# Memory key/value weights through two pairs of raw buffers, and the first two memory query tiles in another product order

## The chip, the cores and the metric

The kernel runs on one core of one Trainium2 chip. The metric is the device time of one execution in microseconds (us). Three executions of the kernel before took 1806.55, 1808.07 and 1809.97 us; the median is 1808.07.

## The reference, cut to what matters

One step of a decoder layer for a prompt of 512 tokens and 8 sample sequences of 8 tokens, so T = 576 token columns in all, D = 1024 features. Three branches (an SSD mixer, block-sparse attention, attention into a memory of 256 tokens) are fed from one input projection, gated, projected and added; a feed-forward block with a short convolution follows. The change lies where the memory branch begins:

```
mkv = (_rmsnorm(mem_prompt, mem_norm_w[l]) @ w_mem_kv[l]).reshape(b_p, n_mem, 2, MEM_HEADS, MEM_HEAD_DIM)
mk_p, mv_p = mkv[:, :, 0], mkv[:, :, 1]
...
y_mem = _mem_attend(qm, mem_k, mem_v)
```

`mem_prompt` has 256 rows; `w_mem_kv` is 1024 x 2048, which is 16 tiles of 1024 x 128. `qm` is a 1024-column part of the input projection of all 576 columns, 8 tiles.

## The kernel before

All dense weights go through one stream of tiles of 1024 x 128 (512 KB), laid out in the order of use. Tile n belongs to parity n % 2, and each parity has one raw buffer (`w_raw`), one pair of split buffers (`w_hi`, `w_lo`) and one PSUM pair (`dps`). fp32 products are made of three reduced-precision ones, high by high, high weight by low activation, and low weight by high activation, 8 contraction steps each.

A tile passes through four queues. SP loads it (`load`, L2543) once the tile before it of the same parity has been split (`w_split`). GpSimd (POOL) waits until TensorE (PE) has finished that earlier tile (`dense_full`) and the load has landed (`w_landed`), writes `w_hi` (L2556), then the difference `w_lo` in four pieces (L2560). PE multiplies (`pe_dense`, L206) in one of two orders: whole, where it waits for `w_hi` alone, makes all products with `w_hi` first (L217) and waits for `w_lo` only then (L222); or in parts, where it waits for both halves and makes the three products step by step (L237).

In the memory stage the 16 key/value tiles (`n_mem` on, called m = 0 to 15 here) are 256 columns wide, so a tile costs PE 24 matmuls where the tiles around it cost 48. There POOL writes only `w_hi` (`split_high`, L2563), and VectorE (DVE) writes `w_lo` (`dve_mem_weight`, L1953), which is what signals `w_split`. Two of these DVE steps stand in the stage before, the block attention's end (`gate1_done` counts its eight merged tiles, L1873): the one of m = 0 behind merged tile 6, that of m = 1 behind merged tile 7. ScalarE (ACT) copies each result out of PSUM (L1984) and issues four loads of `vc` among them (L1988).

Then follow the eight query tiles (`n_qm`, q0 to q7 here), two for each of four heads. `pe_h` (L2104) makes q0 and q1 in parts, with 16 transposes of the memory values between them (`pe_mem_turns`, L1964), before the first head's scores.

Of the kernel before, what the change touches and what calls it, by code (L numbers as in the profile page):

```python
# [16 lines left out]
F32 = mybir.dt.float32  # L17
F32R = mybir.dt.float32r
ALU = mybir.AluOpType
# [4 lines left out]
P = 128  # L24
D = 1024
KT = D // P
SEQ = 512
NB, DT = 8, 8
# [95 lines left out]
def build_program(nc, io):  # L124
    ctx = ExitStack()
    with ctx:
# [3 lines left out]
        def stage_sb(stack, name, shape, dt=F32):  # L130
            return stack.enter_context(nc.sbuf_tensor(name, shape, dt))

        def sem(name):
            return ctx.enter_context(nc.semaphore(name))
# [6 lines left out]
        merged = sb("merged", [P, KT, T])  # L141
        w_raw = sb("w_raw", [P, 2, D])
        w_hi, w_lo = sb("w_hi", [P, 2, D], F32R), sb("w_lo", [P, 2, D], F32R)
        w_taken = sem("w_taken")

        era = ExitStack()
        dt_tok = stage_sb(era, "dt_tok", [P, 2, CH + 1, HEADS])
# [20 lines left out]
        psY = ctx.enter_context(nc.psum_tensor("psY", [P, 512], F32))  # L168


        w_landed = [sem("w_landed0"), sem("w_landed1")]
        w_hi_done = sem("w_hi_done")
        w_split = [sem("w_split0"), sem("w_split1")]
        dense_full = [sem("dense_full0"), sem("dense_full1")]
# [1 line left out]
        cst_in, fea_in, x_in = sem("cst_in"), sem("fea_in"), [sem("x_in0"), sem("x_in1")]  # L176
        out_done = sem("out_done")
        dve_step, act_step = sem("dve_step"), sem("act_step")
        stage_done = [sem("pe_stage"), sem("act_stage"), sem("dve_stage")]

        chains = {}

        ended = [0, 0, 0]

        def stage_end(e, own):

            ended[own] += 1
            count = ended[own]
            e.drain().then_inc(stage_done[own], 1)
            for other in range(3):  # L190
                e.wait_ge(stage_done[other], count)

        def from_one(count):

            return count + 1
# [6 lines left out]
        def slot(n0, u, i=0, nb=0):  # L202

            return (n0 + u) % 2, (n0 + u) // 2 + i * (nb // 2)

        def pe_dense(pe, tile, hi, lo, nk=KT, width=T, ready=None, part=None):  # L206


            par, k0 = tile
            if part is None and ready is None:  # L210
                pe.wait_ge(w_hi_done, k0 * 2 + par + 1)
                pe.wait_ge(dense_free[par], k0)
                spans = [(0, 0, width)] if width <= 512 and width != T else [(0, 0, HALF), (1, HALF, HALF)]
                for k in range(nk):
                    for j, a in enumerate((hi, lo)):
                        for b, c0, cw in spans:
                            pe.matmul(dps[:, par, b, 0:cw], w_hi[:, par, k * P:(k + 1) * P], a[:, k, c0:c0 + cw],  # L217
                                      start=(k == 0 and j == 0), stop=False)
                pe.wait_ge(w_split[par], from_one(k0 + 1))
                for k in range(nk):  # L220
                    for b, c0, cw in spans:
                        mm = pe.matmul(dps[:, par, b, 0:cw], w_lo[:, par, k * P:(k + 1) * P], hi[:, k, c0:c0 + cw],  # L222
                                       start=False, stop=(k == nk - 1))
                mm.then_inc(dense_full[par], 1)
                return
            first, end = part or (0, nk)
            if first == 0:
                pe.wait_ge(w_split[par], from_one(k0 + 1))
                pe.wait_ge(dense_free[par], k0)
            spans = [(0, 0, width)] if width <= 512 and width != T else [(0, 0, HALF), (1, HALF, HALF)]  # L230
            for k in range(first, end):
                if ready:
                    pe.wait_ge(*ready[k])
                wh, wl = w_hi[:, par, k * P:(k + 1) * P], w_lo[:, par, k * P:(k + 1) * P]
                for j, (w, a) in enumerate(((wh, hi), (wh, lo), (wl, hi))):
                    for b, c0, cw in spans:
                        mm = pe.matmul(dps[:, par, b, 0:cw], w, a[:, k, c0:c0 + cw],  # L237
                                       start=(k == 0 and j == 0), stop=(k == nk - 1 and j == 2))
            if end == nk:
                mm.then_inc(dense_full[par], 1)  # L240
# [1648 lines left out]
        kc = ms("kc", [P, NB, 2, MEM])  # L1889
        vc = ms("vc", [P, NB, 2, MEM])  # L1890
        mk = ExitStack()
        stage_sb(mk, "apart_m", [P, 2744])
        mem_hi, mem_lo = (stage_sb(mk, f"mem_{k}", [P, KT, MEM], F32R) for k in ("hi", "lo"))
        memx = stage_sb(mk, "memx", [P, KT, MEM])
        mk.close()
# [57 lines left out]
        def dve_mem_weight(dve, n):  # L1953

            dve.wait_ge(w_hi_done, n + 1)
            par = n % 2
            dve.tensor_tensor(w_lo[:, par, :], w_raw[:, par, :], w_hi[:, par, :].bitcast(F32), ALU.subtract).then_inc(w_split[par], 1)

        def pe_mem(pe):
            pe.wait_ge(mem_lo_ready, mem_at["lo"] + KT)  # L1960
# [52 lines left out]
        n_qm = take(KT)  # L2013
# [90 lines left out]
        def pe_h(pe):  # L2104
            def ahead(h, u, part):
                if h < 4:
                    pe_dense(pe, slot(n_qm, 2 * h + u), xn_hi, xn_lo, part=part)

            ahead(0, 0, (0, KT))
            pe_mem_turns(pe)  # L2110
            ahead(0, 1, (0, KT))
            pe.wait_ge(vmt_copied, 4)
            for h in range(4):
                for u in range(2):
                    par, k0 = slot(n_qm, 2 * h + u)
                    pe.wait_ge(dense_free[par], k0 + 1)
                pe_scores_h(pe, h, 0)
                pe_scores_h(pe, h, 1)
                pe_scores_h(pe, h, "sample")
                ahead(h + 1, 0, (0, KT // 2))  # L2120
                pe_turn_h(pe, h, 0)
                pe_scores_h(pe, h, 2)
                pe_turn_h(pe, h, 1)
                pe_scores_h(pe, h, 3)
                ahead(h + 1, 0, (KT // 2, KT))
                pe_turn_h(pe, h, "sample")
                pe_turn_h(pe, h, 2)
                ahead(h + 1, 1, (0, KT // 2))
                pe_values_s(pe, h)
                pe_turn_h(pe, h, 3)  # L2130
                ahead(h + 1, 1, (KT // 2, KT))
                pe_values_h(pe, h)
                pe_out_s(pe, h)
# [406 lines left out]

        block = ctx.enter_context(nc.Block())
        n_tiles = nstream[0]
        def load(sp, i, par):  # L2543

            sp.wait_ge(w_split[par], from_one(i))
            sp.dma_start(w_raw[:, par, :], io["wstream"][bass.ds(i * 2 + par, 1), :, :].rearrange("o p c -> (o p) c")).then_inc(w_landed[par], 16)
# [1 line left out]
        def load_tile(sp, n):  # L2548
            load(sp, n // 2, n % 2)

        def split(pool, i, par):

            pool.wait_ge(dense_full[par], from_one(i))
            pool.wait_ge(w_landed[par], i * 16 + 16)
            pool.sem_inc(w_taken, 1)
            pool.tensor_scalar(w_hi[:, par, :], w_raw[:, par, :], 1.0, 1.0, ALU.mult, ALU.mult).then_inc(w_hi_done, 1)  # L2556
            pool.wait_ge(w_hi_done, i * 2 + (par + 1))
            for piece in range(4):
                at = slice(piece * D // 4, (piece + 1) * D // 4)
                ins = pool.tensor_tensor(w_lo[:, par, at], w_raw[:, par, at], w_hi[:, par, at].bitcast(F32), ALU.subtract)  # L2560
            ins.then_inc(w_split[par], 1)

        def split_high(pool, i, par):  # L2563

            pool.wait_ge(dense_full[par], from_one(i))
            pool.wait_ge(w_landed[par], i * 16 + 16)
            pool.sem_inc(w_taken, 1)
            pool.tensor_scalar(w_hi[:, par, :], w_raw[:, par, :], 1.0, 1.0, ALU.mult, ALU.mult).then_inc(w_hi_done, 1)

        def split_tile(pool, n):  # L2570
            split(pool, n // 2, n % 2)
# [1 line left out]
        def stream(eng, one, first, end):  # L2573

            if first % 2:
                one(eng, first // 2, 1)
            with eng.Fori((first + 1) // 2, end // 2) as i:
                for par in range(2):
                    one(eng, i, par)
            if end % 2:  # L2580
                one(eng, end // 2, 0)

        @block.sync
        def _(sp):
            sp_load(sp)
            stream(sp, load, 0, n_gate1 + 2)
            sp_pages(sp)
            stream(sp, load, n_gate1 + 2 + NB, n_tiles)
            for written, count in final_waits:
                sp.wait_ge(written, count)  # L2590

        @block.gpsimd
        def _(pool):

            pool.sem_inc(w_split[0], 1)
            pool.sem_inc(w_split[1], 1)
            stream(pool, split, 0, 2)
            norm1.pool(pool)
            stream(pool, split, 2, n_gate1 + 2)
            pool_pages(pool)  # L2600
            stream(pool, split, n_gate1 + 1 + NB, n_mem)
            stream(pool, split_high, n_mem, n_mem + 2 * KT)
            stream(pool, split, n_mem + 2 * KT, n_ffn + 3)
            norm2.pool(pool)
            stream(pool, split, n_ffn + 3, n_tiles)

        @block.tensor
        def _(pe):
# [278 lines left out]
```

## Time and profile before

| | |
|---|---|
| median of three runs | 1808.07 us |
| profiled execution, span | 1812.1 us |
| PE busy | 1742.6 us (96%) |
| DVE, ACT, POOL busy | 924.8, 614.5, 972.8 us |
| mean granted TensorE clock | 0.985 of full speed |
| chain that ended last | PE 89%, DVE 4%, DMA 3%, ACT 2% |

The page shows nothing of the profiled execution outside its span, from the first instruction to the last. Matmuls overlap in the array: one of 256 columns is listed with 0.28 us, but the next one starts 0.12 us later, so costs of PE are read from start to start.

### The profile page before, as it was taken

The page shows a single profiled execution, that of the slowest core. Times are in us where ns is not written, and L with a number is a line of the kernel's source. Part 1 is how long each engine was busy: PE and PEld are TensorE (multiplying, and loading weights), DVE is VectorE, ACT ScalarE, POOL GpSimd, SP SyncE. Part 2 cuts the span into 40 slices and gives each one's busy share as a digit, 9 for nine tenths or more (in the row PEclk, how much of TensorE's full clock was granted, in tenths as well). Part 3 has the DMA queues.
Part 4 walks back from the last instruction along what each step waited for, and adds up shares of the span by engine and source line. Part 5 has one row for each costly group of instructions (what it writes and reads, how often), then busy time and mean ns, then how long its engine had stood idle before and what let it go on. Part 6 is the DMA issues. An engine that isn't in the chain of part 4 may idle for free.

```text
span 1812.1 us, 35702 instructions
## 1 busy us (share of the span) xinstructions
PE 1742.6 (96%) x13888; PEld 1608.6 (89%) x13888; DVE 924.8 (51%) x1558; ACT 614.5 (34%) x1652; POOL 972.8 (54%) x1088
## 2 busy tenths in 40 slices
PE   6999999999999999998999989999999999999997
PEld 6889889899998998885777988779999999999997
DVE  6776677722774334665564731221246761562454
ACT  4355545513554201554442112321024430331231
POOL 4544544555454465211453534226676886886765
PEclk9999999999999999998999999999999999999998
DMA  4113231223213233013786265532222222222222
GB/s 162 62 56 109 98 107 59 97 79 112 95 61 108 96 101 108 25 47 127 268 302 226 81 198 192 192 135 82 82 82 70 82 82 82 82 82 82 82 82 108
DMA packets 53605, 198.48 MB, mean 110 GB/s; under 512 B 6353, under 2 KB 7378, under 8 KB 49874
## 3 DMA queue, kind: packets, MB, share of 16 engines
q1 hardware_dynamic: 41618, 133.36, 22.6%
q10 hardware_dynamic: 7200, 47.81, 7.2%
q0 software_dynamic: 4640, 15.21, 2.4%
q8 instruction: 110, 1.80, 0.4%
q14 instruction: 37, 0.30, 0.0%
HBM read 180.43 MB, written 15.92 MB: 108 GB/s over the span
## 4 chain that ended last, share of the span: by engine, by line
PE 89%; DVE 4%; DMA 3%; ACT 2%; issue 1%; POOL 1%; POOLq 0%; DVEq 0%; SPq 0%; ACTq 0%
PE dps L217 36%; PE dps L222 18%; PE dps L237 16%; DMA w_raw<-wstream_dram 1%; DMA pages<-kv_pages_dram 1%; PE psLE L1645 1%; PE psY L538 1%; PE psLE L588 1%; PE psY L555 1%; PE psY L1366 1%; PE psY L1668 1%; PE psLE L2090 1%; PE psLE L2052 1%; PE psA L1356 1%; PE psY L609 1%
## 5 line engine op out<-in xcount | busy, mean ns | idle before, releaser
L2560 POOL TENSOR_TENSOR w_lo<-w_raw,w_hi 128x256 fp32r<-128x256 f32 x804 | 697.6, 897 | 16.8
L2556 POOL TENSOR_SCALAR w_hi<-w_raw 128x1024 fp32r<-128x1024 f32 x201 | 219.1, 1090 | 663.3 <-PE dps L222 382.6
L217 PE MATMUL dps<-xn_hi,w_hi 128*128 128x288 f32 x1504 | 324.6, 298 | 5.0 <-ACT cbuf L714 4.0
L217 PE MATMUL dps<-xn_lo,w_hi 128*128 128x288 f32 x1504 | 326.2, 299 | 0.0
L217 PEld LDWEIGHTS dps<-xn_hi,w_hi 128*128 128x128 f32 x1504 | 248.4, 191 | 7.9 <-issue 5.3
L217 PEld LDWEIGHTS dps<-xn_lo,w_hi 128*128 128x128 f32 x1504 | 242.6, 190 | 0.0
L222 PE MATMUL dps<-xn_hi,w_lo 128*128 128x288 f32 x1504 | 215.6, 296 | 0.0
L222 PEld LDWEIGHTS dps<-xn_hi,w_lo 128*128 128x128 f32 x1504 | 205.7, 189 | 0.0
L217 PE MATMUL dps<-y_lo,w_hi 128*128 128x288 f32 x808 | 175.0, 298 | 0.0
L217 PE MATMUL dps<-y_hi,w_hi 128*128 128x288 f32 x808 | 173.0, 296 | 0.5 <-POOL w_hi L2556 0.5
L237 PE MATMUL dps<-xn_hi,w_hi 128*128 128x288 f32 x656 | 153.4, 316 | 7.3 <-DVE xn_lo L339 4.1
L237 PE MATMUL dps<-xn_hi,w_lo 128*128 128x288 f32 x656 | 143.4, 301 | 0.0
L237 PE MATMUL dps<-xn_lo,w_hi 128*128 128x288 f32 x656 | 142.8, 300 | 0.0
L237 PEld LDWEIGHTS dps<-xn_hi,w_hi 128*128 128x128 f32 x656 | 106.9, 194 | 31.9 <-issue 23.5
L217 PEld LDWEIGHTS dps<-y_hi,w_hi 128*128 128x128 f32 x808 | 132.3, 190 | 0.9 <-POOL w_hi L2556 0.8
L217 PEld LDWEIGHTS dps<-y_lo,w_hi 128*128 128x128 f32 x808 | 129.6, 189 | 0.0
L222 PE MATMUL dps<-y_hi,w_lo 128*128 128x288 f32 x808 | 116.2, 296 | 0.0
L222 PEld LDWEIGHTS dps<-y_hi,w_lo 128*128 128x128 f32 x808 | 110.6, 189 | 0.0
L237 PEld LDWEIGHTS dps<-xn_lo,w_hi 128*128 128x128 f32 x656 | 108.4, 194 | 0.0
L237 PEld LDWEIGHTS dps<-xn_hi,w_lo 128*128 128x128 f32 x656 | 108.0, 193 | 0.0
L875 DVE SCALAR_TENSOR_TENSOR cout<-cbuf,fea,cout 128x600 f32<-128x600 f32 x96 | 81.9, 854 | 43.1 <-ACT cout L718 40.6
L2469 DVE SCALAR_TENSOR_TENSOR fout<-fin,fea,fout 128x592 f32<-128x592 f32 x44 | 46.7, 1062 | 91.7 <-ACT fout L2455 91.7
(402 smaller groups left out, 2778.8 us busy)
## 6 DMA issues: line engine op xcount, KB each, us to landing
w_raw<-wstream_dram SPq DMA_DIRECT2D x217, 512.0 KB, 3.5
pages<-kv_pages_dram SPq DMA_DIRECT2D x70, 256.0 KB, 3.8
pages<-kv_pages_dram POOLq DMA_DIRECT2D x58, 256.0 KB, 4.0
st_in<-state_t_dram ACTq DMA_DIRECT2D x8, 1024.0 KB, 4.8
ssm_s_dram<-st_in ACTq DMA_DIRECT2D x8, 1024.0 KB, 4.2
kc<-mem_kt_dram ACTq DMA_DIRECT2D x4, 2048.0 KB, 8.8
vc<-mem_v_dram ACTq DMA_DIRECT2D x3, 2048.0 KB, 7.9
h_res<-x_t_dram ACTq DMA_DIRECT2D x1, 2304.0 KB, 9.1
```

Of the source, the lines that this page charges most:

```text
L217: pe.matmul(dps[:, par, b, 0:cw], w_hi[:, par, k * P:(k + 1) * P], a[:, k, c0:c0 + cw], start=(k == 0 and j == 0), stop=False)
L222: mm = pe.matmul(dps[:, par, b, 0:cw], w_lo[:, par, k * P:(k + 1) * P], hi[:, k, c0:c0 + cw], start=False, stop=(k == nk - 1))
L237: mm = pe.matmul(dps[:, par, b, 0:cw], w, a[:, k, c0:c0 + cw], start=(k == 0 and j == 0), stop=(k == nk - 1 and j == 2))
L538: pe.matmul(o, xdt[0:m, h * 64:h * 64 + 64], lv[:, h, :], start=True, stop=not carried)
L555: pe.matmul(psY[:, 256:512], btok[:], xdtd[:], start=True, stop=True).then_inc(y_full, 1)
L588: mm = pe.matmul(psLE[:, half, 0:256], bm[rows, half * 4 + r, :], xds[rows, :], start=True, stop=True)
L609: mm = pe.matmul(gsum[:, c:c + 1], xg_of(G)[:, j, at], ones[:, 0:1], start=(j == 0), stop=(j == halves - 1))
L875: ins = dve.scalar_tensor_tensor(co, cb[:, j:j + CW - PAD], w(j), co, ALU.mult, ALU.add)
L1356: mm = pe.transpose(turn_bank(n)[:, k * P:(k + 1) * P], probs(i)[:, hh, kt * P:(kt + 1) * P], ident)
L2469: link(dve.scalar_tensor_tensor(fo, fb[:, 1:1 + FO], tap_of("fconvw", p, u, 1, FCONV), fo, ALU.mult, ALU.add))
L2556: pool.tensor_scalar(w_hi[:, par, :], w_raw[:, par, :], 1.0, 1.0, ALU.mult, ALU.mult).then_inc(w_hi_done, 1)
L2560: ins = pool.tensor_tensor(w_lo[:, par, at], w_raw[:, par, at], w_hi[:, par, at].bitcast(F32), ALU.subtract)
```

## The change

A second raw pair `w_more` is laid into a stretch of on-chip memory that the memory stage had left unused, and which holds buffers of the block attention until that ends. The 16 key/value tiles use `w_raw` for m = 0, 1, 4, 5, 8, 9, 12, 13 and `w_more` for the others. A load waits for the split of the tile four before it rather than two; the load of m = 2 waits also for `gate1_done` to reach eight, since it is the first to write `w_more`. The first two loads behind the stage, q0 and q1, wait in the same way for m = 12 and 13. The sixteen loads and high splits are written out rather than looped. q0 and q1 are called without `part`, so that they use the whole order. An unused function and its semaphores go.

```diff
+        w_more = stage_sb(mk, "w_more", [P, 2, D])
-        stage_sb(mk, "apart_m", [P, 2744])
+        stage_sb(mk, "apart_m", [P, 2744 - 2 * D])
...
-            dve.tensor_tensor(w_lo[:, par, :], w_raw[:, par, :], w_hi[:, par, :].bitcast(F32), ALU.subtract).then_inc(w_split[par], 1)
+            raw_words = mem_buffer(n - n_mem)[:, par, :]
+            dve.tensor_tensor(w_lo[:, par, :], raw_words, w_hi[:, par, :].bitcast(F32), ALU.subtract).then_inc(w_split[par], 1)
...
-            ahead(0, 0, (0, KT))
+            pe_dense(pe, slot(n_qm, 0), xn_hi, xn_lo)
             pe_mem_turns(pe)
-            ahead(0, 1, (0, KT))
+            pe_dense(pe, slot(n_qm, 1), xn_hi, xn_lo)
...
+        def mem_in_more(m):
+            return m // 2 % 2 == 1
+        def mem_buffer(m):
+            return w_more if mem_in_more(m) else w_raw
+        def load_mem(sp, m):
+            par, i = (n_mem + m) % 2, (n_mem + m) // 2
+            if m // 2 == 0:
+                sp.wait_ge(w_split[par], from_one(i))
+            else:
+                sp.wait_ge(w_split[par], from_one(i - 1))
+            if m // 2 == 1:
+                sp.wait_ge(gate1_done, KT)
+            landed = w_more_landed if mem_in_more(m) else w_landed
+            sp.dma_start(mem_buffer(m)[:, par, :], io["wstream"][n_mem + m]).then_inc(landed[par], 16)
+        def load_behind_mem(sp, u):
+            n = n_mem + 2 * KT + u
+            par, i = n % 2, n // 2
+            sp.wait_ge(w_split[par], from_one(i - 1))
+            sp.dma_start(w_raw[:, par, :], io["wstream"][n]).then_inc(w_landed[par], 16)
...
-        def split_high(pool, i, par):
+        def split_mem(pool, m):
+            par, i = (n_mem + m) % 2, (n_mem + m) // 2
             pool.wait_ge(dense_full[par], from_one(i))
-            pool.wait_ge(w_landed[par], i * 16 + 16)
+            if mem_in_more(m):
+                pool.wait_ge(w_more_landed[par], (m // 4 + 1) * 16)
+            else:
+                pool.wait_ge(w_landed[par], (i - m // 2 + m // 4 + 1) * 16)
             pool.sem_inc(w_taken, 1)
-            pool.tensor_scalar(w_hi[:, par, :], w_raw[:, par, :], 1.0, 1.0, ALU.mult, ALU.mult).then_inc(w_hi_done, 1)
+            pool.tensor_scalar(w_hi[:, par, :], mem_buffer(m)[:, par, :], 1.0, 1.0, ALU.mult, ALU.mult).then_inc(w_hi_done, 1)
...
-            stream(sp, load, n_gate1 + 2 + NB, n_tiles)
+            stream(sp, load, n_gate1 + 2 + NB, n_mem)
+            for m in range(2 * KT):
+                load_mem(sp, m)
+            for u in range(2):
+                load_behind_mem(sp, u)
+            stream(sp, load, n_mem + 2 * KT + 2, n_tiles)
...
-            stream(pool, split_high, n_mem, n_mem + 2 * KT)
-            stream(pool, split, n_mem + 2 * KT, n_ffn + 3)
+            for m in range(2 * KT):
+                split_mem(pool, m)
+            stream(pool, split_behind_mem, n_mem + 2 * KT, n_ffn + 3)
```

`split_behind_mem` is `split` with the count of landings lowered by the four tiles of each parity that landed in `w_more`.

## Rows read from the trace of the kernel before

**Rows 1.** Page, the chain that ended last: shares of the span by engine.

```profile
PE 89%; DVE 4%; DMA 3%; ACT 2%; issue 1%; POOL 1%; POOLq 0%; DVEq 0%; SPq 0%; ACTq 0%
```

**Rows 2.** Busy by stretch: engines (instructions), granted clock, DMA share, GB/s.

```profile
1035.60:1089.00 53.40, 47.73 (x386) 45.94 (x384) 20.09 (x17) 5.76 (x15) 17.97 (x17) 1.00 0.56 180
```

**Rows 3.** Chain of waits, memory stage: start us, us, what.

```profile
1048.98 0.05 SPq L2546
...
1049.13 3.46 DMA w_raw<-wstream_dram
...
1052.76 1.05 POOL w_hi L2568
...
1053.83 1.24 DVE w_lo L1957
```

**Rows 4.** Waits by releaser, 1030 to 1112 us: total us, times, longest.

```profile
PE dps L217 <- POOL w_hi L2568: 5.6, 7, 1.6
```

**Rows 5.** Timeline PE, first matmuls of m = 0, 2, 3 and 15.

```profile
1035.62 0.28 PE L217 MATMUL dps<-mem_hi,w_hi 128*128 128x256 f32 x1
...
1041.30 0.28 PE L217 MATMUL dps<-mem_hi,w_hi 128*128 128x256 f32 x1
...
1044.13 0.32 PE L217 MATMUL dps<-mem_hi,w_hi 128*128 128x256 f32 x1
...
1085.88 0.39 PE L217 MATMUL dps<-mem_hi,w_hi 128*128 128x256 f32 x1 [0.20 <-POOL w_hi L2568]
```

**Rows 6.** Timeline PE, the longest stall inside the memory stage.

```profile
1079.75 0.39 PE L217 MATMUL dps<-mem_hi,w_hi 128*128 128x256 f32 x1 [1.58 <-POOL w_hi L2568]
```

**Rows 7.** Timeline DVE: low split of m = 0, then the eighth merge.

```profile
1031.18 1.21 DVE L1957 TENSOR_TENSOR w_lo<-w_raw,w_hi 128x1024 fp32r<-128x1024 f32 x1
...
1036.67 1.05 DVE L1873 TENSOR_TENSOR merged<-merged,cst_b 128x576 f32<-128x576 f32 x1
```

**Rows 8.** DMA issues, 985 to 1112 us, then 1061.8 to 1062 us: KB, us to landing.

```profile
w_raw<-wstream_dram SPq DMA_DIRECT2D x26, 512.0 KB, 3.6
vc<-mem_v_dram ACTq DMA_DIRECT2D x4, 512.0 KB, 5.5
...
w_raw<-wstream_dram SPq DMA_DIRECT2D x1, 512.0 KB, 6.0
```

**Rows 9.** DMA issues at 944.4, a burst's first, and 946.1 to 946.7 us, its last.

```profile
pages<-kv_pages_dram SPq DMA_DIRECT2D x1, 256.0 KB, 3.2
...
pages<-kv_pages_dram SPq DMA_DIRECT2D x1, 256.0 KB, 4.1
```

**Rows 10.** Timeline PE: first matmuls of q0, of the transposes and of q1.

```profile
1091.28 0.53 PE L237 MATMUL dps<-xn_hi,w_hi 128*128 128x288 f32 x2 [2.30 <-POOL w_lo L2560]
...
1099.30 0.60 PE L1972 MATMUL psA<-cst,memx 128*128 128x128 f32 x4
...
1100.96 0.51 PE L237 MATMUL dps<-xn_hi,w_hi 128*128 128x288 f32 x2
```

**Rows 11.** Timeline POOL: high and low split of q0.

```profile
1087.32 1.05 POOL L2556 TENSOR_SCALAR w_hi<-w_raw 128x1024 fp32r<-128x1024 f32 x1 [1.49 <-DMA w_raw<-wstream_dram]
1088.46 2.77 POOL L2560 TENSOR_TENSOR w_lo<-w_raw,w_hi 128x256 fp32r<-128x256 f32 x4
```

**Rows 12.** Busy by stretch, as Rows 2: inside q0, then two other stretches.

```profile
1092.30:1095.00 2.70, 2.70 (x13) 2.70 (x13) 0.00 (x0) 0.00 (x0) 2.62 (x4) 0.50 1.04 385
...
1382.00:1386.00 4.00, 3.74 (x16) 3.65 (x17) 3.97 (x7) 2.43 (x5) 3.58 (x3) 0.57 0.00 0
825.00:836.00 11.00, 10.64 (x46) 6.81 (x46) 4.93 (x14) 5.02 (x16) 0.00 (x0) 0.53 0.00 0
```

**Rows 13.** Timeline PE: the stall just ahead of 1382.26 us.

```profile
1382.26 0.85 PE L237 MATMUL dps<-xn_hi,w_hi 128*128 128x288 f32 x2 [1.56 <-DVE xn_lo L339]
```

**Rows 14.** Chain of waits, q1 and what follows it.

```profile
1101.21 6.39 PE dps L237 x48
1107.62 0.66 ACT qh L2141
```

**Rows 15.** Timeline ACT, the last `vc` load of the stage.

```profile
1072.26 0.33 ACTq L1988 DMA_DIRECT2D vc<-mem_v_dram  x1
```

More of the change, by code:

```diff
@@ L143, in build_program @@
         w_hi, w_lo = sb("w_hi", [P, 2, D], F32R), sb("w_lo", [P, 2, D], F32R)
-        w_taken = sem("w_taken")
         era = ExitStack()
@@ L168, in build_program @@
         psY = ctx.enter_context(nc.psum_tensor("psY", [P, 512], F32))
+        w_taken = sem("w_taken")
         w_landed = [sem("w_landed0"), sem("w_landed1")]
+        w_more_landed = [sem("w_more_landed0"), sem("w_more_landed1")]
         w_hi_done = sem("w_hi_done")
@@ L178, in build_program @@
         dve_step, act_step = sem("dve_step"), sem("act_step")
-        stage_done = [sem("pe_stage"), sem("act_stage"), sem("dve_stage")]
         chains = {}
[L183 to L191, printed above, removed]
         def from_one(count):
@@ L2549, in load_tile, with split @@
             load(sp, n // 2, n % 2)
-        def split(pool, i, par):
+        def split(pool, i, par, elsewhere=0):
             pool.wait_ge(dense_full[par], from_one(i))
-            pool.wait_ge(w_landed[par], i * 16 + 16)
+            pool.wait_ge(w_landed[par], i * 16 + (16 - elsewhere * 16))
             pool.sem_inc(w_taken, 1)
@@ L2561, in split, with split_behind_mem @@
             ins.then_inc(w_split[par], 1)
-        def split_high(pool, i, par):
+        def split_mem(pool, m):
+            par, i = (n_mem + m) % 2, (n_mem + m) // 2
             pool.wait_ge(dense_full[par], from_one(i))
-            pool.wait_ge(w_landed[par], i * 16 + 16)
+            if mem_in_more(m):
+                pool.wait_ge(w_more_landed[par], (m // 4 + 1) * 16)
+            else:
+                pool.wait_ge(w_landed[par], (i - m // 2 + m // 4 + 1) * 16)
             pool.sem_inc(w_taken, 1)
-            pool.tensor_scalar(w_hi[:, par, :], w_raw[:, par, :], 1.0, 1.0, ALU.mult, ALU.mult).then_inc(w_hi_done, 1)
+            pool.tensor_scalar(w_hi[:, par, :], mem_buffer(m)[:, par, :], 1.0, 1.0, ALU.mult, ALU.mult).then_inc(w_hi_done, 1)
+        def split_behind_mem(pool, i, par):
+            split(pool, i, par, elsewhere=KT // 2)
         def split_tile(pool, n):
@@ L2601, in _ @@
             stream(pool, split, n_gate1 + 1 + NB, n_mem)
-            stream(pool, split_high, n_mem, n_mem + 2 * KT)
-            stream(pool, split, n_mem + 2 * KT, n_ffn + 3)
+            for m in range(2 * KT):
+                split_mem(pool, m)
+            stream(pool, split_behind_mem, n_mem + 2 * KT, n_ffn + 3)
             norm2.pool(pool)
-            stream(pool, split, n_ffn + 3, n_tiles)
+            stream(pool, split_behind_mem, n_ffn + 3, n_tiles)
         @block.tensor
```

## The prediction

> **What bounds the kernel now.** I read the chain that ended last first: PE holds 89% of it [rows 1], so for most of the span only shorter or earlier PE work moves the end. Next, the busy times by stretch for the one place that the change touches. From 1035.6 to 1089.0 PE is busy 47.7 of 53.4 us at the full granted clock of 1.00 (2.4 GHz) [rows 2]: 5.7 us of idle PE, which is no clock loss. Then the chain inside this stretch, for what ended the idle time: it leaves PE and runs round a loop of DMA, POOL's `w_hi`, DVE's `w_lo`, SP's next load [rows 3]. One turn, from a load's start to the next load's start of the same parity, is 3.46 + 0.17 + 1.05 + 0.02 + 1.24 + 0.16 = 6.1 us, and it feeds one tile of that parity, while PE needs two tiles' time. That is 2 x 2.84 = 5.68 us, since m = 0 to 2 follow one another without a stall, (1041.30 - 1035.62) / 2 = 2.84 [rows 5]. The loop is longer, so PE waits for `w_hi`: 5.6 us in 7 stalls [rows 4], none over 1.58 [rows 6].
>
> What the stalls cost is better taken from starts, because the listed idle time leaves out the array's pipeline. From m = 2 to m = 15 there are 13 tiles, 13 x 2.84 = 36.9 us, and they took 1085.88 - 1041.30 = 44.6 [rows 5]. **Loss in the stage: 7.7 us.**
>
> Behind it PE waits 2.30 us for q0's `w_lo` [rows 10], which POOL makes only from 1088.46 on, because its `w_hi` had waited 1.49 us for the load [rows 11]. Then q0 itself is slow: from its first matmul to the transposes 1099.30 - 1091.28 = 8.0 us [rows 10], where q1, the same 48 matmuls, takes 6.39 [rows 14]; the granted clock is 0.50 (1.2 GHz) in the middle of q0 [rows 12]. So 1.6 us are lost to the clock.
>
> **The change, part by part.** *Loads through two pairs.* A load now waits for the split of the tile four before. Its buffer is free two tiles (5.7 us) earlier than before, while the turn was only 0.4 us too long, or 3.0 too long with the slowest landing of 6.0 us against the 3.46 of that turn [rows 3, 8]. So from m = 3 on I count no stall. The bound on that is what remains without DMA in the loop: POOL starts after the tile two before has ended and needs 1.05 of the 2.84 us, then DVE 1.24 [rows 3], and `w_lo` is due only two thirds into the tile. Gain 7.7 us.
>
> *The new wait at m = 2.* The load of m = 2 was free to start when DVE had split m = 0, at 1031.18 + 1.21 = 1032.4. Now it waits for the eighth merge, which ends at 1036.67 + 1.05 = 1037.72 [rows 7]. SP then needs 0.15 us to start the transfer [rows 3]: 1037.87. With the median landing of 3.6 us [rows 8], 0.17 to POOL, 1.05 for `w_hi` and 0.02 to PE, m = 2 can start at 1042.71, where it started at 1041.30 [rows 5]: **a new stall of 1.4 us**, plus 0.1 for a slower first matmul behind a stall (0.39 against 0.28 us [rows 5, 6]). Queued behind SP's waiting load are those of m = 3, 4 and 5, and all later ones. m = 4 is free since 1032.4, m = 3 and 5 by about 1039, so four loads of 512 KB leave nearly together, with a `vc` load beside them. What the last ones land late by does not count at first: m = 3 is not due at PE before 1042.7 + 2.84 = 45.5, and m = 5 not before 1051.
>
> How fast m = 2 itself lands with others behind it the trace does not show for 512 KB. The nearest rows are a burst of eight page loads on one queue: the first lands in 3.2, the last in 4.1 us [rows 9]. A load beside another queue's `vc` load took up to 6.0 [rows 8]. I take 3.6, as the first of a burst was not slowed, with ends of 3.2 and 6.2 (0.2 more for a third transfer): stall 1.0 to 4.0 us.
>
> The Trainium skill speaks against my choice here. Its page "DMA: Bandwidth & Descriptors", section "Queues, rings and completion order", says that an engine takes descriptors in ring order, but that data descriptors carry no barrier, so a later one may finish first. By that the load of m = 2 need not be ahead of m = 3 and 4, and would lie at the long end; the page-load burst, whose first landed soonest, does not agree so far.
>
> *q0 and its loads.* The loads of q0 and q1 now leave after m = 12 and 13, some 5 us earlier. So POOL starts q0 when m = 14 has ended, that is about when m = 15 starts, and has both halves 1091.23 - 1087.32 = 3.9 us later [rows 11], 1.1 us into q0. In the whole order PE waits for `w_hi` alone, ready before m = 15 ends, and needs `w_lo` after 32 of 48 matmuls, 4.3 us into q0: 3.2 us of cover. The idle 2.30 us go. With no idle time ahead of q0 I also expect no fall of the clock, so its 1.6 us go. From starts: m = 15 to q1 was 1100.96 - 1085.88 = 15.08 us [rows 5, 10], and becomes 2.84 + 6.39 + 1.66 (the transposes, 1100.96 - 1099.30) = 10.89. **Gain 4.2 us.** The whole order costs nothing of its own (48 matmuls either way).
>
> *q1.* POOL makes its halves after q0's, ready 2 x 3.9 = 7.8 us after m = 15's start, when PE is still in q0: no wait before, none now.
>
> *Written-out loads and splits, moved semaphores.* One POOL and one SP instruction chain per tile as before; the loop's bookkeeping costs under 0.2 us on each handoff (0.17 from landing to POOL [rows 3]), and only m = 2's handoff is on the path. I take nothing, within -0.2 and +0.2.
>
> *After q1.* q1's end releases ACT's copy and with it the first head [rows 14]. The operands that might come too late there move along: the last `vc` load leaves behind m = 10's copy, before at 1072.26 [rows 15], then some 4 us earlier, and lands in about 5.5 [rows 8], far ahead of the first head. So what q1 gains, the end gains.
>
> Sum: -7.7 + 1.4 + 0.1 - 4.2 = **-10.4 us**. It stands against a span of 1812.1 us, which is 4.0 above the median 1808.07; no term scales with that difference, so I take it off the median: **1797.7 us**.
>
> **The rivals.** (1) *The burst delays m = 2.* Its bytes share the engines with m = 3 and 4 and it lands in 6.2 us: gain 10.4 - 2.6 = 7.8, time 1800.3. For it, the loads beside `vc`; against it, the page bursts. (2) *The clock falls at m = 2.* A stall of 1.56 us at 1382 [rows 13] was followed by a stretch at 0.57 [rows 12], but stalls up to 1.58 in the memory stage were not [rows 2, 6]. It costs what q0's fall did, 1.6 us: 1799.3. The skill's page "TensorE: Matmul & The Clock Gate", section "What's actually happening", says that recent activity decides the clock; by that rule one stall among dense tiles leaves most of the recent work in place and speaks for no fall, and the stage's own stalls agree. (3) *The gain is swallowed.* If the first head, or a stage after it, waits for something that does not move, the time stays at 1808. The chain against it: PE alone leads from q1 into the heads [rows 14]; for it, only that I traced no further than that. (4) *Slower: the clock falls at m = 2 and stays down.* At half clock every tile costs 2.84 us more; from 10.4 / 2.84 = 3.7 tiles on, some 21 us at half clock, the kernel is slower than before, and with all 14 tiles low it takes 1797.7 + 39.8 = 1837.5. The longest low stretch that I found is 11 us at 0.53 (825 to 836) [rows 12], in work less dense than these tiles.
>
> **How the numbers follow.** Chances: forecast 0.68, rival 1 0.10, rival 2 0.12, rival 3 0.06, rival 4 0.04. No change means within 0.2%, 3.6 us, about what a measurement of this kernel can tell. Faster is then 0.68 + 0.10 + 0.12 = 0.90, same 0.06, slower 0.04. The range: at best a landing in 3.2 us gives 1797.3; the three runs before spread 1.5 to 1.9 about their median, so the low end is 1795. Upward it takes in rivals 1 and 2 together, 1801.9, and ends at 1802.5; rivals 3 and 4 are left out.
>
> **What would show it.** Right: matmul starts 2.84 us apart from m = 2 to m = 15; one stall of about 1.4 us, before m = 2; the load of m = 2 leaving SP at about 1037.9 of a like span; no idle PE between m = 15 and q0; q0 in 6.4 us at clock 1.00; m = 0 to q1 in 1035.62 to about 1090.6 in place of 1100.96. Wrong: waits of PE for `w_hi` that still come from DMA landings, a wait for q0's `w_lo`, or a head stage that starts earlier and ends where it did.

## The result and the profile after

Six runs of the changed kernel took 1788.47 to 1798.33 us, median 1796.57; the kernel before, beside them, 1808.18 (six runs). The ratio is 0.9927, with an interval of 0.9907 to 0.9947. On the 1808.07 of before that is 1794.9 us: faster, as forecast, by 13.2 us rather than 10.4, and 0.1 under the low end of the range, 1795.0; by the two medians it is 11.6. Twelve later runs of the same kernel gave 1797.47 against 1807.06, a ratio of 0.9950 (0.9932 to 0.9969), 9.0 us, or 1799.0 on the same 1808.07. The two intervals overlap, so the size is known to some 3 us only, and the question is what moves by that much.

The profiled execution has a span of 1795.8 us and a time of 1797.52: what lies around a span is 1.7 us. PE's first matmuls of m = 0, 2, 3 and 15, as in [rows 5]:

```profile
1032.99 0.28 PE L208 MATMUL dps<-mem_hi,w_hi 128*128 128x256 f32 x1
...
1039.89 0.39 PE L208 MATMUL dps<-mem_hi,w_hi 128*128 128x256 f32 x1 [1.07 <-POOL w_hi L2591]
...
1042.83 0.28 PE L208 MATMUL dps<-mem_hi,w_hi 128*128 128x256 f32 x1
...
1076.91 0.28 PE L208 MATMUL dps<-mem_hi,w_hi 128*128 128x256 f32 x1
```

One stall stands in the stage, before m = 2. From m = 2 to m = 15 it is 37.0 us, 13 x 2.84 and 0.1 for the first matmul, where it was 44.6 [rows 5]. The next rows are q0, the transposes and q1, as in [rows 10]:

```profile
1079.75 0.43 PE L208 MATMUL dps<-xn_hi,w_hi 128*128 128x288 f32 x2
...
1086.14 0.60 PE L1965 MATMUL psA<-cst,memx 128*128 128x128 f32 x4
...
1087.80 0.51 PE L208 MATMUL dps<-xn_hi,w_hi 128*128 128x288 f32 x2
```

q0 begins one tile's 2.84 us after m = 15, with no idle time, and takes 6.39 us. From m = 0 to q1 the kernel needs 1087.80 - 1032.99 = 54.8 us, where it needed 1100.96 - 1035.62 = 65.3 [rows 5, 10]: **10.5 us less, against 10.4 forecast**. The chain of waits through the new stall, in order of time, shows what it is:

```profile
1034.05 0.99 DVE merged L1864
1035.04 0.02 issue
1035.05 0.02 SPq L2551
1035.07 0.03 issue
1035.10 3.52 DMA w_more<-wstream_dram
1038.62 0.03 POOLq L2590
1038.65 0.14 issue
1038.79 1.05 POOL w_hi L2591
1039.85 0.04 issue
1039.89 2.16 PE dps L208 x16
```

The reader sees the wait for the eighth merge, then one transfer, then POOL and PE. The chain runs through PE alone from there to the first head.

The profiled spans differ by 16.3 us, 5.8 more than the stage. m = 0 starts 2.6 us earlier, ahead of anything that the change touches, and 3.2 us are gained behind it. Behind the stage this goes with two falls of the clock that the kernel before had alone, that at 1382 [rows 12] and one at 1761. Ahead of it both profiles have falls that the other lacks. A second profile of the kernel before (below) had its m = 0 at 1030.64 rather than 1035.62, so such shifts need no change of the kernel. Busy by stretch of the first profile of the kernel before (the granted clock is the third number from the end):

```profile
141.00:147.00 6.00, 5.83 (x31) 5.55 (x32) 3.03 (x8) 3.78 (x9) 3.34 (x4) 0.72 0.49 177
820.00:836.00 16.00, 13.51 (x70) 8.65 (x68) 8.62 (x22) 8.35 (x24) 0.00 (x0) 0.68 0.00 0
853.00:867.00 14.00, 10.65 (x174) 8.31 (x174) 5.31 (x15) 4.81 (x14) 6.92 (x11) 0.88 0.61 196
955.00:975.00 20.00, 16.00 (x275) 10.32 (x279) 12.39 (x37) 10.63 (x35) 8.15 (x13) 1.00 0.73 247
```

and of the second:

```profile
141.00:147.00 6.00, 6.00 (x48) 5.70 (x46) 2.58 (x7) 3.34 (x9) 2.91 (x4) 1.00 0.54 187
820.00:836.00 16.00, 12.79 (x86) 9.24 (x85) 10.66 (x27) 10.38 (x29) 0.00 (x0) 0.89 0.04 7
853.00:867.00 14.00, 13.80 (x228) 9.73 (x229) 8.98 (x20) 5.96 (x18) 6.04 (x9) 1.00 0.66 217
955.00:975.00 20.00, 16.44 (x228) 11.29 (x228) 10.99 (x28) 7.00 (x23) 5.98 (x9) 0.83 0.41 143
```

The first lacks 1.7, 3.4 and 1.7 us of the clock in the first three stretches against the second (0.28 of 6 us, 0.21 of 16, 0.12 of 14), and the second lacks 3.4 against the first in the last (0.17 of 20). That is 3.4 of the 5.0 us by which the first had its m = 0 later; what the rest is stays open. The changed kernel's profile has falls of its own in the last two stretches (0.88 and 0.83), so the falls explain 1.7 of its 2.6 us.

### The profile page after: what moved, and what is told of

The parts are those of the page before. It is cut to its first block, busy times and chain, and to the rows that moved or that the text cites. A ratio compares the mean times of both kernels' runs of the same rounds, so it can differ in the third digit from the quotient of the medians.

```text
span 1795.8 us, 35606 instructions
## 1 busy us (share of the span) xinstructions
PE 1732.6 (96%) x13888; PEld 1601.0 (89%) x13888; DVE 924.3 (51%) x1558; ACT 614.2 (34%) x1652; POOL 980.4 (55%) x1088
## 4 chain that ended last, share of the span: by engine, by line
PE 90%; DVE 3%; DMA 2%; ACT 2%; issue 1%; POOL 1%; SPq 0%; DVEq 0%; POOLq 0%; ACTq 0%
PE dps L208 38%; PE dps L213 19%; PE dps L228 15%; DMA pages<-kv_pages_dram 2%; PE psY L529 1%; PE psLE L1636 1%; PE psLE L579 1%; PE psY L546 1%; PE psY L1357 1%; PE psLE L2083 1%; PE psY L1659 1%; PE psLE L2045 1%; PE psA L1347 1%; PE psY L600 1%; PE psA L1645 1%
## 5 line engine op out<-in xcount | busy, mean ns | idle before, releaser
L2579 POOL TENSOR_TENSOR w_lo<-w_raw,w_hi 128x256 fp32r<-128x256 f32 x804 | 704.7, 906 | 16.8
L208 PE MATMUL dps<-xn_lo,w_hi 128*128 128x288 f32 x1536 | 328.8, 296 | 0.0
L208 PEld LDWEIGHTS dps<-xn_hi,w_hi 128*128 128x128 f32 x1536 | 249.2, 190 | 7.4 <-issue 4.9
L228 PE MATMUL dps<-xn_lo,w_hi 128*128 128x288 f32 x624 | 135.2, 299 | 0.0
L228 PEld LDWEIGHTS dps<-xn_hi,w_hi 128*128 128x128 f32 x624 | 100.8, 192 | 29.3 <-issue 23.7
L2462 DVE SCALAR_TENSOR_TENSOR fout<-fin,fea,fout 128x592 f32<-128x592 f32 x44 | 39.8, 904 | 94.4 <-ACT fout L2448 94.4
```

The lines of the kernel that those rows point to most:

```text
L2462: link(dve.scalar_tensor_tensor(fo, fb[:, 1:1 + FO], tap_of("fconvw", p, u, 1, FCONV), fo, ALU.mult, ALU.add))
```

## The experiments

**The change again, for its spread.** No edit.

> The changed kernel once more, unchanged, for its spread: of its first six runs four took 1795.8 to 1798.3 us and two 1788.5 and 1788.9. Theory A (the change is worth the worked-out 10.5 us in its stage, and whatever else a run shows is its spread): the profile shows 54.8 us from m = 0 to q1 again, runs come in both groups again, and the two groups differ outside this stage. Rival B (the second pair of buffers brings 8 us more in a later or earlier stage in some runs): the lower group's profile is shorter in one stage that uses the weight stream. Rival C (clock falls alone make the spread): the granted clock of the lower group's runs is higher than that of the others.

1797.47 us, from 1792.85 to 1801.30. The stage is as in the first profile, m = 0 to the transposes 53.2 us in both, and PE's listed idle time at m = 2 is 1.09 us, there 1.07. None of these twelve came near 1788, so that part of theory A, both groups again, failed. But of 31 runs of the kernel before, taken beside this experiment and the next three, three lay at 1795.87 to 1798.00 under a median of 1807.06, and two of twelve of the pairs alone, below, at 1788.1. So low runs belong to no one of these kernels (against B). The clock of those three, 0.988 to 0.990, is also that of runs at 1802 to 1807 (against C, for the large step; the runs above 1808 have 0.986 to 0.988, which fits C for the small ones).

**The two pairs alone.**

```diff
-            pe_dense(pe, slot(n_qm, 0), xn_hi, xn_lo)
+            ahead(0, 0, (0, KT))
...
-            pe_dense(pe, slot(n_qm, 1), xn_hi, xn_lo)
+            ahead(0, 1, (0, KT))
```

> The two pairs of raw buffers alone; q0 and q1 in parts as before, so that q0 waits for both halves. Theory A: the memory stage is as in the changed kernel (one stall of about 1.2 us at m = 2, then 2.84 us per tile); q0 waits for its low half, ready about 1.4 us after the end of m = 15. Total about 9.0 us less than before where the clock holds at that stall, 7.4 less where it falls as it did in the kernel before (q0 then 8.0 in place of 6.4 us). Rival (the order of q0 does all of the 4.2 us at its place, the loads none): 6.3 us less, with 2.3 us of wait and a slow q0 as before.

1798.31 us, ratio 0.9951 (0.9929 to 0.9973): 8.8 us by the medians. PE at m = 15, q0 and the transposes:

```profile
1074.48 0.28 PE L208 MATMUL dps<-mem_hi,w_hi 128*128 128x256 f32 x1
...
1078.85 0.54 PE L228 MATMUL dps<-xn_hi,w_hi 128*128 128x288 f32 x2 [1.37 <-POOL w_lo L2579]
...
1085.33 0.60 PE L1965 MATMUL psA<-cst,memx 128*128 128x128 f32 x4
```

q0 waits 1.37 us for its low half, as worked out, and then takes 6.48: the clock did not fall behind this stall. m = 0 to the transposes is 54.75 us, 8.9 less than before. So the loads alone remove q0's slow clock too. They cut the idle time ahead of q0 from 2.30 to 1.37 us and took away the stalls ahead of that; which of the two kept the clock up is not shown, since a stall of 1.56 us was followed by a fall elsewhere [rows 12, 13].

**The whole order alone**, in the kernel before.

```diff
-            ahead(0, 0, (0, KT))
+            pe_dense(pe, slot(n_qm, 0), xn_hi, xn_lo)
...
-            ahead(0, 1, (0, KT))
+            pe_dense(pe, slot(n_qm, 1), xn_hi, xn_lo)
```

> The whole order of q0 and q1 alone; one pair of raw buffers as before. Theory A: the memory stage keeps its 44.6 us from m = 2 to m = 15; q0 starts as soon as m = 15 ends, since its high half was ready 0.5 us earlier, and finds its low half; no clock fall: 4.2 us less than before. Rival (q0's late load is what cost, not the order): q0 still waits, less than 1 us gained.

1801.62 us, ratio 0.9969 (0.9950 to 0.9988): 5.4 us by the medians. PE at m = 15, q0 and the transposes:

```profile
1077.13 0.38 PE L217 MATMUL dps<-mem_hi,w_hi 128*128 128x256 f32 x1 [0.23 <-POOL w_hi L2568]
...
1080.07 0.43 PE L217 MATMUL dps<-xn_hi,w_hi 128*128 128x288 f32 x2
...
1086.46 0.60 PE L1972 MATMUL psA<-cst,memx 128*128 128x128 f32 x4
```

From m = 15 to the transposes 9.33 us, before 13.42 [rows 5, 10]: 4.1 less, as expected. The rest of this profile's 5.0 us lies in the stage (m = 2 to m = 15 43.7 us), where landings scatter. The two parts do not add up, 8.9 + 4.1 against 10.5, since the loads alone already take 0.9 us of q0's wait and its 1.6 us of slow clock.

**The second pair one turn later**, so that no tile waits for the merge.

```diff
-            return m // 2 % 2 == 1
+            return m >= 4 and m // 2 % 2 == 0
...
-            if m // 2 == 0:
+            if m // 2 < 2:
...
-            if m // 2 == 1:
+            if m // 2 == 2:
                 sp.wait_ge(gate1_done, KT)
```

q0 and q1 then wait for the split of m = 14 and 15, and the counts of landings follow.

> The changed kernel with the second pair used first by m = 4 and 5 rather than by m = 2 and 3, so that no load waits for the eighth merge while its tile is due: m = 2 loads into the first pair once m = 0 is split, as in the kernel before. Theory A (the stall at m = 2 is the load's wait for the merge): no stall at m = 2, 2.84 us per tile from m = 0 to m = 15, 53.6 us from m = 0 to q1, 1.2 us less than the changed kernel. Rival (something else at the stage's start costs it): the stall stays or moves to m = 4, and the time is that of the changed kernel.

1794.08 us, ratio 0.9921 (0.9893 to 0.9950): 13.0 us less than before by the medians, 3.4 less than the twelve runs of the change. All sixteen tiles follow one another at 2.84 us; m = 2 and m = 3:

```profile
1038.03 0.28 PE L208 MATMUL dps<-mem_hi,w_hi 128*128 128x256 f32 x1
...
1040.87 0.28 PE L208 MATMUL dps<-mem_hi,w_hi 128*128 128x256 f32 x1
```

m = 0 to the transposes is 51.8 us, 1.3 less than with the change: the stall was the load's wait. This is the best kernel here by its stage. The other 2 us of the medians are spread, and this profile, span 1785.6, shows of which kind. In the feed-forward stage PE is busy without a gap and at full clock in both kernels, yet does more in the same time. First this kernel, then the changed one:

```profile
1400.00:1700.00 300.00, 300.00 (x2310) 300.00 (x2310) 145.76 (x145) 81.92 (x258) 233.41 (x242) 1.00 0.27 86
```

```profile
1400.00:1700.00 300.00, 300.00 (x2252) 300.00 (x2251) 139.73 (x141) 79.56 (x249) 232.11 (x236) 1.00 0.26 83
```

2310 matmuls against 2252. A tile of 48 takes 6.23 us here, from one tile's low products to the next's:

```profile
1385.44 0.51 PE L208 MATMUL dps<-xn_hi,w_hi 128*128 128x288 f32 x2 [1.03 <-ACT fin L2439]
...
1502.01 2.24 PE L213 MATMUL dps<-y_hi,w_lo 128*128 128x288 f32 x16
...
1508.24 2.24 PE L213 MATMUL dps<-y_hi,w_lo 128*128 128x288 f32 x16
...
1734.72 0.53 PE L228 MATMUL dps<-y_hi,w_hi 128*128 128x288 f32 x2 [1.94 <-POOL w_lo L2579]
```

and 6.40 in the changed kernel:

```profile
1500.56 2.29 PE L213 MATMUL dps<-y_hi,w_lo 128*128 128x288 f32 x16
1506.96 2.29 PE L213 MATMUL dps<-y_hi,w_lo 128*128 128x288 f32 x16
```

The short pitch begins at the stall that ends at 1385.44 and ends with the one at 1734.72. Over 349 us at 2.5% it is worth some 8.8 us, about the step by which the low runs lie below the others.

**Stops in the feed-forward stage**, to see whether a restart sets the pitch.

```diff
+                    if p % 2 == 0:
+                        par, k0 = slot(PAIRS[p - 1], 1)
+                        pe.wait_ge(dense_free[par], k0 + 1)
                     pe_pair(pe, p)
```

> The changed kernel, with PE made to stop and start again ahead of every second pair of the feed-forward stage (it waits there until the tile just before has been copied out). Theory A2 (the low group of runs is set by how PE starts again after a stall: in the profile of a low run, PE left a 1.0 us stall at 1385 at 6.24 us for 48 matmuls in place of 6.40 and kept that to the next stall at 1735): stretches between two stops run at one pitch each, some at 6.24 and some at 6.40 us. Rival (the pitch is a property of the whole execution): one pitch in all stretches. In both, the time is above that of the changed kernel, by ten stops of 1 to 4 us each and what the clock falls by them: 1810 to 1840 us.

1817.85 us. PE's first two stops in the stage and the low products between them:

```profile
1386.82 0.85 PE L208 MATMUL dps<-xn_hi,w_hi 128*128 128x288 f32 x2 [7.27 <-ACT fin L2442]
1393.05 2.24 PE L213 MATMUL dps<-xn_hi,w_lo 128*128 128x288 f32 x16
1399.29 2.24 PE L213 MATMUL dps<-xn_hi,w_lo 128*128 128x288 f32 x16
1405.53 2.24 PE L213 MATMUL dps<-xn_hi,w_lo 128*128 128x288 f32 x16
1411.77 2.24 PE L213 MATMUL dps<-xn_hi,w_lo 128*128 128x288 f32 x16
1415.11 0.53 PE L208 MATMUL dps<-xn_hi,w_hi 128*128 128x288 f32 x2 [1.10 <-ACT fin L2442]
1419.47 2.29 PE L213 MATMUL dps<-xn_hi,w_lo 128*128 128x288 f32 x16
```

6.24 us a tile after the stop of 7.27 us, 6.40 from the next stop on, and so behind all nine stops of 1.10. One execution has both pitches, so the pitch is not a property of the whole execution, and the rival falls. In this stage, where nothing but a stop interrupts equal matmuls, it changed at a stop, as A2 has it. Which restart gives which is open. The 1.10 us stops all gave the long one, so it is no even draw, and a stall of 1.03 us in the profile above gave the short one.

A2 is too narrow, though, for the pitch changes without a stop too. In the first profile of the changed kernel PE has no idle time listed from 409 to 432 us. Behind a stretch at half clock, 413.8 to 417.1, it runs short:

```profile
419.56 2.24 PE L213 MATMUL dps<-y_hi,w_lo 128*128 128x288 f32 x16
...
425.80 2.24 PE L213 MATMUL dps<-y_hi,w_lo 128*128 128x288 f32 x16
```

This is 6.24 us a tile. Five groups of matmuls of other shapes follow, and from 428.88 on the pitch is the long one. Nine of the ten profiles have such a short stretch ahead of 430 us, the first one of the kernel before at 85 to 91. What sets the low run apart is that its stretch lasted 349 us.

**Each kernel once more.** No edits. These and the stops above ran on another chip than the first four experiments.

> The changed kernel once more, one look, for its spread. Theory A2: 53.2 us from m = 0 to the transposes as before; 1793 to 1801 us with 6.40 us a tile in the feed-forward stage, or 1786 to 1790 with 6.24.

> The kernel whose second pair serves m = 4 and 5 first, one more look. 51.8 us from m = 0 to the transposes again; 1791 to 1798 us with 6.40 us a tile in the feed-forward stage, 1781 to 1788 with 6.24 (theory A2).

> The kernel before, one more look. 63.7 us from m = 0 to the transposes, give or take 1.5 for the landings; 1804 to 1812 us with 6.40 us a tile in the feed-forward stage, 1795 to 1800 with 6.24 (theory A2).

1795.15, 1794.83 and 1805.02 us; m = 0 to the transposes 53.0, 51.8 and 63.1 us; all three at 6.40 us a tile in the feed-forward stage. The stage's times come again to 0.6 us, whatever the whole run does. The second of them and the low run profiled above are one kernel at the two pitches, with spans of 1793.2 and 1785.6 us. None of the three fell among the low runs, so that every low run owes its place to the pitch is argued from the size of the step, and shown once. One more run of the kernel before, beside these, took 1816.15 us at a mean clock of 0.983, 3.7 above the slowest of the 31; what slowed it was not traced.

## Why the prediction was right and where it failed

*The loads*: right. 7.7 us of stalls went, and no landing stops PE behind m = 2.

*The wait at m = 2*: 1.4 forecast, 1.2 measured (1039.89 - 1035.83 - 2.84). The load left at once behind the merge and landed in 3.5 us, as the lower part of the bounds had it. The burst was there, and cost the third and fourth of the four (6.9 and 7.6 us), not the first, and they landed in the order of issue; DMA issues from 1035.1 and from 1036 us, KB and us to landing:

```profile
w_more<-wstream_dram SPq DMA_DIRECT2D x1, 512.0 KB, 3.5
...
w_raw<-wstream_dram SPq DMA_DIRECT2D x1, 512.0 KB, 6.9
```

So rival 1 fell, and with it the use that I made of "DMA: Bandwidth & Descriptors" (the Trainium skill, "Queues, rings and completion order"): a later transfer may finish first by that page, but here the first of a burst on one queue was not held up. The burst of page loads on which the forecast leaned [rows 9] is four loads in the trace, not eight; its first landed soonest all the same.

*q0*: right in each term. m = 15 to q1 took 10.89 us, the forecast to the hundredth; the order alone gave 4.1 of the 4.2.

*The clock at m = 2* (rival 2): no fall; the granted clock is 1.00 from 1033 to 1081. *After q1*: passed on; the first head starts 0.83 us of ACT's copy after q1, as before. Rivals 3 and 4 fell with it. Rival 4's price was too high: in the slow part of q0 of the kernel before, matmuls start 0.24 us apart, against 0.13 at full clock, so a tile at half clock would cost by estimate some 2.3 us more, not 2.84.

*The range* failed, by 0.1 us, and the step that failed is its term for the scatter: "the three runs before spread 1.5 to 1.9 about their median, so the low end is 1795". Three runs that happened to agree were too few. The 31 of the same kernel lie from 11.2 below to 5.4 above their median, and the six of the changed kernel from 8.1 below to 1.8 above theirs. Two of these six, at 1788.5 and 1788.9, were 8.6 us lower on average than the rest. The other four average 1797.2 us, 11.1 less than the 1808.3 of the six of before, which is near the stage's 10.5; with the two low ones the ratio gives 13.2. That two of six were low, where none of the next twelve was, is chance as far as the runs show, and so is a miss by 0.1.

The trace of before held one of the two sources: falls of the clock that come in one execution and not in another, worth 1.7 to 3.4 us each in the stretches shown above, which I listed as a danger at m = 2 only and not as scatter of every run. The other, the matmul pitch, is worth 8.8 us in the one low run with a profile, and stood in no row that I read. The two low runs that made the ratio have no profile, so that they owe their place to the pitch stays argued.

## What to carry to other kernels

Where a load waits for the buffer that it refills, compare one turn of that loop with the work of the buffers between; a second pair gains the time by which the turn is the longer, and this shows first where a tile is little work. Give memory that is borrowed from an earlier stage to the first tile that is not yet due, not to the next one. Take the scatter of a range from many runs, or from sources in the trace, not from three times that happen to agree.

## What the runs showed of the hardware

The same gapless matmuls at the same granted clock of 1.00 run at two pitches, 6.24 and 6.40 us for 48 of 288 columns. In the feed-forward stage the pitch changed only at stops of PE; elsewhere it also changed without idle time, behind a stretch at half clock and behind matmuls of other shapes. What sets it is open. POOL's high split, 1.05 us for the other tiles of this profile, took 2.02 us beside DVE's low split of the tile before, which had begun 0.12 us earlier:

```profile
1040.06 2.02 POOL L2591 TENSOR_SCALAR w_hi<-w_more 128x1024 fp32r<-128x1024 f32 x1 [0.22 <-DMA w_more<-wstream_dram]
```

Two more profiles of this kernel have 1.99 and 1.97 us at the same place. It cost nothing, since PE began that tile at 1042.83, without idle time ahead of it.
